# MLA head projections of a two-block model: rotations over both token tiles, a second query bank, the last heads' transposes moved behind the first scores

## The chip, the cores and the metric

One NeuronCore of one Trainium2 chip. The number reported is the device time of one execution in microseconds (us); several executions are summarised by their median. Lower is better.

## What is computed

The kernel computes two transformer blocks in a row on 256 tokens of width 1024, all in fp32. The second block has two layers: layer 0 with a sparse attention mixer (NSA), layer 1 with multi-head latent attention (MLA), and each layer ends in a mixture of 16 experts. The change is in layer 1's mixer:

```python
c_q = mix_cols[..., :MLA_Q_RANK]
c_kv = mix_cols[..., MLA_Q_RANK:MLA_Q_RANK + MLA_KV_RANK]
k_rope = mix_cols[..., MLA_Q_RANK + MLA_KV_RANK:]
q = (rms_norm_2(c_q, q_norm) @ w_uq).reshape(B, S, H, MLA_NOPE + MLA_ROPE)
q = jnp.concatenate([q[..., :MLA_NOPE], apply_rope(q[..., MLA_NOPE:], cos_m, sin_m)], -1)
kv = (rms_norm_2(c_kv, kv_norm) @ w_ukv).reshape(B, S, H, MLA_NOPE + MLA_V)
k_nope, v = kv[..., :MLA_NOPE], kv[..., MLA_NOPE:]
k_rope = apply_rope(k_rope[:, :, None, :], cos_m, sin_m)
k = jnp.concatenate([k_nope, jnp.broadcast_to(k_rope, (B, S, H, MLA_ROPE))], -1)
...
s = jnp.einsum('bqhd,bkhd->bhqk', qb, k) * scale
p = masked_softmax(s, mask)
```

The query rank is 256, the key/value rank 128, there are 12 heads, and of a head's 96 query and key columns the last 32 are rotated by position. After the mixer come an output projection with a residual and a layer norm, then the experts, whose weights (96 halves of 1 MB) are streamed from HBM.

## The kernel before

The program is written engine by engine: `tensor_program` (TensorE, PE in the profile), `vector_program` (VectorE, DVE), `scalar_program` (ScalarE, ACT), `pool_program` (GpSimd, POOL) and `sync_program` (the queue that issues the DMAs, SP). Each engine runs its list in order; semaphores tie the lists together. The 256 tokens are two tiles of 128 (t = 0, 1). PSUM has eight banks. `Banks.work` hands banks 0 to 3 out in turn to the named stages; `Banks.plan` names the banks. A stage's bank is claimed by TensorE (it waits until the last user's copy out of it is done), filled, and then emptied by DVE or ACT (`evac`).

The stretch around the change, in TensorE's order:

1. Stages `m` and `xq2` (L1674 to L1684): layer 1's input projection. `m` gives for each tile 416 columns (256 of c_q, 128 of c_kv, 32 of the key to be rotated), copied to the buffer `pm`; `xq2` is the query of the memory attention.
2. The root wait. ACT squares and sums both parts of both tiles of `pm` (L2972), DVE turns four sums into means (L2495), POOL takes the two inverse roots one after the other (L3029), and DVE multiplies the four parts by them (L2500). Only then does DVE rotate the key columns of tile 0 and of tile 1 (`rope`, L1849 to L1855, six instructions of 128x16 each).
3. Stages `cq` and `ck` (L1686 to L1694): six transposes, all four of `cq` into one bank; DVE copies both banks out with the gains (L2508, L1763).
4. `keep_on(psum[4], 7)` (L1726): seven matmuls of a constant on a constant, whose result nobody reads.
5. The head projections. Twelve heads are three parts of four. Step n (0 to 5) is part n // 2, the query for even n and key and value for odd n: `project(n)` fills banks `mp{n}`, one for each tile. For the query ACT copies tile 0 out and DVE tile 1, and DVE then rotates 4 heads x 16 column pairs of each tile (six instructions of 128x64 for each tile, L2525). For the key and value ACT does the copies (L2989, L2990), and POOL lays the rotated key beside every head (L3141). `turn_heads(n)` transposes the 96 columns of four heads back into banks `mt{n}`, two of them; ACT and DVE empty one each (`turned_heads`, 96x512). The transposes of step n - 2 come behind `project(n)`, those of steps 4 and 5 at the end. DVE and ACT also cut four pieces of the next weight matrix `ob0` into a high and a low half (`cast` on ACT L2597, then `cut` on DVE L1779), two before the loop and two at n == 1.
6. `attention(2)`: 8 turns of the loop over `c` for 12 MLA heads and 4 memory heads, and two turns to drain. In a turn TensorE makes four score tiles, transposes the probabilities of the turn before (`turn_probs`), and multiplies by the values. DVE adds the mask and takes the row minimum (`masks`), ACT takes the exponents, DVE the inverse sums, POOL scales the rows (L3039). Before the first score TensorE waits until banks 0 to 3 are empty. In the turn c == 1 it has another `keep_on(psum[7], 4)`.

The order on SP matters too. The first 23 expert halves of layer 1 are loaded ahead, each where its buffer comes free; of these the halves from n == 5 wait for s_pv 72, that is for the values of the last MLA heads (L903), and from n == 12 for the cut of `ob1` (L907). Once the experts run, a half is loaded whenever one has been used (L931).

## Time and profile before

| | us |
|---|---|
| median of 3 runs (lowest, highest) | 1025.46 (1024.38, 1026.41) |
| span of the profiled execution, first to last instruction | 1018.3 |
| median less that span | 7.2 |
| PE, DVE, ACT, POOL busy in the span | 977.9, 553.7, 410.1, 107.9 |
| HBM traffic over the span | 286 GB/s |

No time of the profiled execution is given beside its span. What lies around the span is taken as the 7.2 us by which the median is longer.

How to read it: a row of a timeline gives the start in us from the start of the span, the time in us until the group's last instruction ended, the engine, the source line, the operation, what is written and read with the shape, and how many instructions were merged (x4). In brackets stand the idle time just before it and who ended that. The table of windows gives for each stretch its length, then for PE, PEld (weight loads), DVE, ACT and POOL the busy time and the count of instructions, then TensorE's granted clock (1.00 is 2.4 GHz, 0.50 is 1.2 GHz), the share of the 16 DMA engines' time in which they were busy, and GB/s. Successive DVE instructions overlap, so their starts lie closer together than their durations say.

### The profile page before, as it was taken

The page shows a single profiled execution, that of the slowest core. Times are in us where ns is not written, and L with a number is a line of the kernel's source. Part 1 is how long each engine was busy: PE and PEld are TensorE (multiplying, and loading weights), DVE is VectorE, ACT ScalarE, POOL GpSimd, SP SyncE. Part 2 cuts the span into 40 slices and gives each one's busy share as a digit, 9 for nine tenths or more (in the row PEclk, how much of TensorE's full clock was granted, in tenths as well). Part 3 has the DMA queues.
Part 4 walks back from the last instruction along what each step waited for, and adds up shares of the span by engine and source line. Part 5 has one row for each costly group of instructions (what it writes and reads, how often), then busy time and mean ns, then how long its engine had stood idle before and what let it go on. Part 6 is the DMA issues. An engine that isn't in the chain of part 4 may idle for free.

```text
span 1018.3 us, 15420 instructions
## 1 busy us (share of the span) xinstructions
PE 977.9 (96%) x5850; PEld 666.7 (65%) x5850; DVE 553.7 (54%) x1201; ACT 410.1 (40%) x817; POOL 107.9 (11%) x143
## 2 busy tenths in 40 slices
PE   7999999999999999899999999989999999999995
PEld 7977899999886889777634334337777734343432
DVE  5766656676447744774523434366665613334374
ACT  5465456556436445683312122124474302221222
POOL 0721001111001100150001000000132001000000
PEclk9999999999999999999999999999999999999998
DMA  9882596556354543709999999997367999999994
GB/s 328 208 259 83 167 294 218 181 181 228 130 206 165 163 153 127 309 3 361 406 422 421 409 420 421 420 403 252 107 275 281 406 408 420 410 421 421 421 416 160
DMA packets 96686, 292.30 MB, mean 287 GB/s; under 512 B 11150, under 2 KB 48190, under 8 KB 73566
## 3 DMA queue, kind: packets, MB, share of 16 engines
q1 hardware_dynamic: 96606, 291.24, 75.2%
q8 instruction: 49, 0.80, 0.3%
q14 instruction: 31, 0.25, 0.1%
HBM read 289.98 MB, written 1.25 MB: 286 GB/s over the span
## 4 chain that ended last, share of the span: by engine, by line
PE 79%; DVE 8%; DMA 6%; ACT 3%; issue 2%; POOL 1%; SPq 0%; DVEq 0%; POOLq 0%; ACTq 0%
PE ps L1056 37%; PE ps L1517 16%; PE ps L1557 10%; DMA w<-in_moe_w_up 3%; DMA arena<-in_moe_w_up 3%; DVE yTr L2417 2%; PE ps L1165 2%; PE ps L1195 2%; PE ps L1176 2%; PE ps L1488 1%; PE ps L999 1%; DVE plo L1779 1%; PE ps L1567 1%; PE ps L1361 1%; PE ps L1605 1%
## 5 line engine op out<-in xcount | busy, mean ns | idle before, releaser
L1779 DVE TENSOR_TENSOR plo<-w,phi 128x1024 fp32r<-128x1024 f32 (+3 forms) x147 | 178.0, 1229 | 130.5 <-ACT phi L2597 130.2
L2597 ACT CAST phi<-w 128x1024 fp32r<-128x1024 f32 (+3 forms) x147 | 148.6, 1033 | 132.0 <-PE ps L1056 125.7
L2417 DVE SCALAR_TENSOR_TENSOR yTr<-ps,small,yTr 32x512 fp32r<-32x512 f32 x112 | 83.7, 748 | 179.6 <-ACT yTr L2896 177.9
L1517 PE MATMUL ps<-w,arena 128*64 128x512 f32 x464 | 135.6, 594 | 1.3 <-DMA w<-in_moe_w_up 1.3
L1056 PE MATMUL ps<-hTr,phi 128*128 128x256 f32 x472 | 131.5, 279 | 0.3 <-DVE yTr L1961 0.3
L1056 PE MATMUL ps<-hTr,plo 128*128 128x256 f32 x472 | 130.9, 277 | 0.0
L1056 PE MATMUL ps<-yTr,phi 128*128 128x256 f32 x472 | 130.9, 277 | 0.0
L1056 PE MATMUL ps<-phi,hTr 128*128 128x512 f32 (+2 forms) x240 | 93.8, 391 | 1.3 <-issue 0.7
L1056 PE MATMUL ps<-phi,yTr 128*128 128x512 f32 (+2 forms) x240 | 93.7, 390 | 0.7 <-DVE hTr L1771 0.7
L1056 PEld LDWEIGHTS ps<-hTr,phi 128*128 128x128 f32 x472 | 88.8, 188 | 0.6 <-issue 0.4
L1056 PEld LDWEIGHTS ps<-hTr,plo 128*128 128x128 f32 x472 | 88.9, 188 | 0.0
L1056 PEld LDWEIGHTS ps<-yTr,phi 128*128 128x128 f32 x472 | 88.7, 188 | 0.0
L1517 PE MATMUL ps<-arena 128*64 128x512 f32 x272 | 82.9, 595 | 1.5 <-DMA arena<-in_moe_w_up 1.5
L1517 PEld LDWEIGHTS ps<-w,arena 128*64 128x64 f32 x464 | 42.1, 137 | 62.8 <-issue 61.9
L1557 PE MATMUL ps<-w,ring 128*64 128x512 f32 (+1 forms) x296 | 78.6, 559 | 1.2 <-ACT ring L2920 0.7
L2896 ACT ACTIVATE yTr<-ps,small 128x512 fp32r<-128x512 f32 (+1 forms) x62 | 37.1, 674 | 98.6 <-PE ps L1557 90.5
L3029 POOL TENSOR_TENSOR small<-small 128x1 f32<-128x1 f32 (+1 forms) x18 | 11.5, 636 | 468.3 <-DVE small L1824 354.1
L1056 PE MATMUL ps<-plo,hTr 128*128 128x512 f32 (+2 forms) x144 | 55.4, 385 | 0.0
L1557 PEld LDWEIGHTS ps<-w,ring 128*64 128x64 f32 x296 | 26.9, 137 | 40.2 <-issue 37.3
L1056 PEld LDWEIGHTS ps<-phi,hTr 128*128 128x128 f32 x240 | 45.2, 188 | 11.8 <-issue 2.2
L1056 PEld LDWEIGHTS ps<-phi,yTr 128*128 128x128 f32 x240 | 45.2, 188 | 10.1 <-issue 1.4
L1517 PEld LDWEIGHTS ps<-arena 128*64 128x64 f32 x272 | 25.5, 137 | 39.9 <-issue 38.9
(372 smaller groups left out, 1729.8 us busy)
## 6 DMA issues: line engine op xcount, KB each, us to landing
w<-in_moe_w_up SPq DMA_DIRECT2D x31, 1024.0 KB, 18.0
w<-in_moe_w_down SPq DMA_DIRECT2D x30, 1024.0 KB, 17.4
w<-in_moe_w_gate SPq DMA_DIRECT2D x26, 1024.0 KB, 14.0
w<-in_w_up SPq DMA_DIRECT2D x22, 1024.0 KB, 7.8
arena<-in_moe_w_up SPq DMA_DIRECT2D x19, 1024.0 KB, 15.5
arena<-in_moe_w_gate SPq DMA_DIRECT2D x14, 1024.0 KB, 21.6
arena<-in_moe_w_down SPq DMA_DIRECT2D x13, 1024.0 KB, 18.7
w<-in_w_out SPq DMA_DIRECT2D x6, 2048.0 KB, 10.3
```

Of the source, the lines that this page charges most:

```text
L999: e.matmul(bank[:, 0:width], ident, mask if width == 256 else ident, start=True, stop=True)
L1056: ins_ = e.matmul(o, l[a], r[b], start=first and i == 0, stop=last and i == 2, skip_group_check=group)
L1165: ins_ = e.matmul(psum[2 * (u % 2) + j["half"]][:, q * 256:q * 256 + w], lq, kk, start=True, stop=True)
L1176: ins_ = e.transpose(bk[:, o * 128:o * 128 + 128], prob(j["J"])[:, c:c + 128], ident)
L1195: ins_ = e.matmul(ob[hp:hp + 64, t * 128:t * 128 + 128], *m[o], start=(o == 0), stop=(o == len(m) - 1))
L1517: ins_ = e.matmul(bank[64 * ee:64 * ee + 64, :], xg[:, k, o:o + 64], half_view(i, kind, p, ee, ab)[:, c, :], start=(k == 0), stop=(k == 7))
L1557: ins_ = e.matmul(bank[64 * ee:64 * ee + 64, :], turned[:, o:o + 64], down_view(i, p, ee, f, hf)[:, at], start=(f == 0), stop=(f == 3))
L1779: e.tensor_tensor(plo[:, 0:m], slots[u % 3][:, j * m:j * m + m], phi[:, 0:m].bitcast(F32), ALU.subtract).then_inc(s_cut)
L2417: ins_ = e.scalar_tensor_tensor(y_parts[t][other, part], psum[2 + hf][own_, :], slot_gate[own_, p:p + 1], y_parts[t][own_, part].bitcast(F ...
L2597: e.copy(pieces[p % 4][0][:, 0:m], slots[u % 3][:, j * m:j * m + m]).then_inc(s_cast)
L2896: ins_ = e.mul(y_parts[part][:, hf * 512 + at.start:hf * 512 + at.stop], bank[:, :], slot_gate[:, p:p + 1])
L3029: e.tensor_tensor(dst, dst, half_pow[:, 0:dst.shape[-1]], ALU.pow).then_inc(s_rstd)
```

## The change

- `cq` gets two banks, one for each half of the query rank. ACT empties the first, DVE the second; before, DVE emptied both halves. All later `work` stages move on by one bank.
- The key's rotation moves in front of the four multiplications by the inverse roots, and it is done over both tiles at once (`rope_tiles`, six instructions of 128x32). Tile 0's two multiplications stay on DVE, each waiting for its own root alone; tile 1's go to ACT. Before them ACT runs one Exp on a column, so that the Exp table is loaded there.
- Query rotations of a part go over both tiles at once (six instructions of 128x128 for twelve of 128x64), with scratch in `ring`.
- `keep_on(psum[4], 7)` becomes `keep_on(psum[4], 1)`, and the wait for `ck` moves to `project(1)`. `keep_on(psum[7], 4)` stays in layer 0's attention and is dropped from layer 1's.
- `turn_heads(4)` and `turn_heads(5)` move into the attention's turn c == 0, behind the first four score tiles, into banks 6, 7 and 4, 5; their copies on DVE stand behind `inverse_sums(0)`, on ACT behind the exponents of the second two tiles.
- The second pair of `ob0` pieces is cut at n == 0.

```diff
-        trq = [ar(64).rearrange("p (h d) -> p h d", h=4) for _ in range(4)]
+        trq = [ring[:, a:a + 128].rearrange("p (t h d) -> p t h d", t=2, h=4) for a in range(0, 512, 128)]
...
-        for stage, n in (("cq", 1), ("ck", 1)):
+        for stage, n in (("cq", 2), ("ck", 1)):
...
-        for n in (4, 5):
-            B.work(f"mt{n}", 2)
+        B.plan("mt4", 2, [6, 7])
+        B.plan("mt5", 2, [4, 5])
...
+                    if a == 2 and c == 0:
+                        turn_heads(4)
+                        turn_heads(5)
...
-                    if a and c == 1:
+                    if a == 1 and c == 1:
                         keep_on(psum[7], 4)
...
-            bk = claim("cq", 0)
             e.wait_ge(s_mnorm, 4)
-            for q in range(4):
-                ins_ = e.transpose(bk[:, q * 128:q * 128 + 128], pm[:, q % 2, (q // 2) * 128:(q // 2) * 128 + 128], ident)
-            ins_.then_inc(B.sem_full("cq", 0))
+            for c in range(2):
+                bk = claim("cq", c)
+                for t in range(2):
+                    ins_ = e.transpose(bk[:, t * 128:t * 128 + 128], pm[:, t, c * 128:c * 128 + 128], ident)
+                ins_.then_inc(B.sem_full("cq", c))
...
-            keep_on(psum[4], 7)
+            keep_on(psum[4], 1)
             e.wait_ge(*loaded("uq"))
             e.wait_ge(*loaded("ukv"))
-            await_empty("cq", "ck")
+            await_empty("cq")
             for n in range(6):
+                if n == 1:
+                    await_empty("ck")
                 project(n)
                 if n >= 2:
                     turn_heads(n - 2)
-            turn_heads(4)
-            turn_heads(5)
             attention(2)
...
+            def rope_tiles(x1, x2, lo, hi_, tmp, heads=0):
+
+                c, s = trig[:, 0, 0:2, lo:hi_], trig[:, 1, 0:2, lo:hi_]
+                if heads:
+                    c, s = (a.unsqueeze(2).broadcast_to([128, 2, heads, hi_ - lo]) for a in (c, s))
                 settle()
                 e.tensor_tensor(tmp[0], x1, c, ALU.mult)
                 e.tensor_tensor(tmp[1], x2, s, ALU.mult)
...
-            e.wait_ge(s_rstd, root.n)
             for t in range(2):
-                for n, (c0, w) in enumerate(((0, 256), (256, 128))):
-                    e.tensor_scalar(pm[:, t, c0:c0 + w], pm[:, t, c0:c0 + w], rsm[:, n, t:t + 1], None,
-                                    ALU.mult).then_inc(s_mnorm)
-            tr = [a[:, 0:16] for a in tmp4]
-            for t in range(2):
-                rope(pm[:, t, 384:400], pm[:, t, 400:416], t, 8, 24, [], tr).then_inc(s_mrope)
-                e.wait_ge(s_mrope, t + 1)
...
+                e.wait_ge(*B.empty("m", t))
+            tr = [a[:, 0:32].rearrange("p (t d) -> p t d", t=2) for a in tmp4]
+            rope_tiles(pm[:, :, 384:400], pm[:, :, 400:416], 8, 24, tr).then_inc(s_mrope)
+            for n, (c0, w) in enumerate(((0, 256), (256, 128))):
+                e.wait_ge(s_rstd, root.n - 1 + n)
+                e.tensor_scalar(pm[:, 0, c0:c0 + w], pm[:, 0, c0:c0 + w], rsm[:, n, 0:1], None,
+                                ALU.mult).then_inc(s_mnorm)
+            evac("cq", 1, cqT[:, 1, :], B.ap("cq", 1)[:, 0:256], colv[:, QN + 1:QN + 2])
             evac("ck", 0, ckT[:, 0, :], B.ap("ck", 0)[:, 0:256], colv[:, KN:KN + 1])
...
                 for t in range(2):
                     e.wait_ge(*B.empty(f"mp{n}", t))
-                    ins_ = rope(qk[:, t, :, 64:80], qk[:, t, :, 80:96], t, 8, 24, [4], trq)
-                    ins_.then_inc(s_qr)
-                    e.wait_ge(s_qr, 2 * part + t + 1)
+                rope_tiles(qk[:, :, :, 64:80], qk[:, :, :, 80:96], 8, 24, trq, 4).then_inc(s_qr)
...
+            e.wait_ge(s_msq, 4)
+            e.activation(table, ident[:, 0:1], ACT.Exp)
+            for n, (c0, w) in enumerate(((0, 256), (256, 128))):
+                e.wait_ge(s_rstd, 13 + n)
+                e.mul(pm[:, 1, c0:c0 + w], pm[:, 1, c0:c0 + w], rsm[:, n, 1:2]).then_inc(s_mnorm)
             evac("xq2", 0, xqT2, B.ap("xq2", 0)[:, :].rearrange("p (c t) -> p c t", c=2), -0.125,
                  used(first_piece("m1") + 3, 1))
+            evac("cq", 0, cqT[:, 0, :], B.ap("cq", 0)[:, 0:256], colv[:, QN:QN + 1])
...
-                if n == 1:
+                if n == 0:
                     cast(p0 + 2, p0 + 4)
```

## Rows read from the trace of the kernel before

**Rows 1.** Busy time, granted clock, DMA share and GB/s of three stretches to the end.

```profile
751.90:770.30 18.40, 17.36 (x156) 13.35 (x154) 14.10 (x69) 14.83 (x62) 9.57 (x11) 1.00 0.17 70
770.30:813.30 43.00, 41.65 (x244) 34.09 (x246) 22.95 (x64) 15.01 (x28) 3.96 (x5) 1.00 0.97 393
813.30:1002.00 188.70, 184.75 (x876) 71.05 (x872) 75.92 (x145) 35.31 (x60) 3.55 (x2) 1.00 1.01 412
```

**Rows 2.** Timeline of SP: the first DMA issue at the attention's end.

```profile
770.29 0.33 SPq L859 DMA_DIRECT2D arena<-in_moe_w_gate  x1
```

**Rows 3.** Timeline of the root wait, up to the first projection.

```profile
717.63 0.24 DVE L2495 TENSOR_SCALAR small<-small 128x2 f32<-128x2 f32 x2 [1.29 <-ACT ring L2972]
...
718.83 0.70 POOL L3029 TENSOR_TENSOR small<-small 128x2 f32<-128x2 f32 x1 [0.16 <-issue]
...
719.56 1.01 DVE L2500 TENSOR_SCALAR arena<-arena,small 128x256 f32<-128x256 f32 x4 [1.69 <-POOL small L3029]
...
720.14 0.28 PE L1056 MATMUL ps<-hTr,plo 128*128 128x256 f32 x1
...
720.72 0.63 PE L1689 MATMUL ps<-cst,arena 128*128 128x128 f32 x4 [0.29 <-DVE arena L2500]
...
720.95 1.98 ACT L2597 CAST phi<-w 128x1024 fp32r<-128x1024 f32 x2
...
721.40 3.19 PE L999 MATMUL ps<-cst 128*128 128x256 f32 x14
...
722.00 0.88 DVE L2508 TENSOR_SCALAR arena<-ps,colv 128x256 f32<-128x256 f32 x2
...
723.19 2.44 DVE L1779 TENSOR_TENSOR plo<-w,phi 128x1024 fp32r<-128x1024 f32 x2
```

**Rows 4.** The key/value weights: their issue on SP, and its time to landing.

```profile
716.37 0.34 SPq L777 DMA_DIRECT2D w<-in_mla_w_ukv  x1
...
w<-in_mla_w_ukv SPq DMA_DIRECT2D x1, 768.0 KB, 4.4
```

**Rows 5.** Timeline of TensorE in the projections and transposes.

```profile
724.42 2.75 PE L1704 MATMUL ps<-w,arena 128*128 128x384 f32 x8
...
736.21 0.64 PE L1723 MATMUL ps<-cst,arena 128*96 128x128 f32 x4 [1.15 <-DVE arena L1763]
...
742.87 0.64 PE L1723 MATMUL ps<-cst,hT 128*96 128x128 f32 x4 [0.41 <-DVE arena L1763]
743.35 1.91 PE L1723 MATMUL ps<-cst,arena 128*96 128x128 f32 x16
```

**Rows 6.** Timeline of DVE: evacuation, rotation, evacuation.

```profile
732.89 0.55 DVE L1761 COPY hT<-ps 128x384 f32<-128x384 f32 x1
...
733.36 0.21 DVE L1849 TENSOR_TENSOR arena<-hT,small 128x64 f32<-128x64 f32 x1
...
735.47 0.69 DVE L1763 TENSOR_SCALAR arena<-ps 96x512 f32<-96x512 f32 x1
```

**Rows 7.** Timeline of DVE in layer 0's rotation, instructions of 128x96.

```profile
385.75 0.25 DVE L1849 TENSOR_TENSOR small<-arena,small 128x96 f32<-128x96 f32 x1
```

**Rows 8.** Timeline of the attention's first two turns, TensorE and POOL.

```profile
746.08 2.00 PE L1165 MATMUL ps<-arena 96*128 96x128 f32 x12 [0.83 <-DVE arena L1761]
...
749.59 1.04 POOL L3039 TENSOR_TENSOR ring<-ring,small 128x512 f32<-128x512 f32 x1 [0.28 <-DVE small L1893]
...
751.48 0.60 PE L1176 MATMUL ps<-cst,ring 128*128 128x128 f32 x4
```

**Rows 9.** Timeline of ACT where the Exp table was loaded early on.

```profile
56.21 1.28 ACT L2720 ACT_TABLE_LOAD   x1
57.51 0.20 ACT L2720 ACTIVATE small<-cst 128x1 f32<-128x1 f32 x1
```

**Rows 10.** Busy time and granted clock of two stretches at the end.

```profile
1008.00:1012.00 4.00, 0.00 (x0) 0.00 (x0) 3.84 (x7) 2.84 (x10) 1.22 (x3) 1.00 0.02 6
1012.00:1018.30 6.30, 0.00 (x0) 0.00 (x0) 2.36 (x4) 0.00 (x0) 0.40 (x1) 0.59 0.48 177
```

29 lines of the change are left out of this document (17 added, 12 removed).

## The prediction

> **What bounds the kernel now.** I read the table of windows first, to find what sets the end. From 813.3 to 1002 us the DMA engines are busy for the whole stretch (share 1.01, 412 GB/s), and from 770.3 to 813.3 nearly so (0.97), while from 751.9 to 770.3 they are almost idle (0.17) [rows 1]. So the end is a stream of expert weights that starts at one instant and runs at the rate of the DMA engines. The timeline of SP gives that instant: the first issue after the idle stretch is at 770.29, and in the code it waits for the values of the last MLA heads (s_pv 72, L903) [rows 2]. All later issues of the stream wait for work behind that attention, so an attention that ends x us earlier should move the whole tail by x. In the stretch before it there is DMA idle time on one side and a chain over three engines on the other: whatever shortens the chain is worth its full length.
>
> The chain is read from the timeline, in three pieces: the root wait up to the first projection at 724.42 [rows 3, 5], the projections, in which TensorE twice waits for a DVE evacuation (1.15 us before 736.21, 0.41 before 742.87) [rows 5], and the attention from 746.08, whose second turn puts its last transposes at 751.48 [rows 8].
>
> **The change, part by part.** Times are those of the profiled execution; I compute new instants on the same axis.
>
> *Root wait.* Now DVE multiplies from 719.56, when the second root is there (718.83 + 0.70), to 720.57, and the transposes start at 720.72 although TensorE had issued its last product at 720.14 [rows 3]. The rotation stands behind the multiplications and holds the first evacuation of `cq` until 722.00. In the new order DVE rotates both tiles between 717.87 and about 718.7, under POOL's roots, and multiplies tile 0's two parts at about 718.7 and 719.6. ACT multiplies tile 1's. The Exp table load begins behind the squares at 717.63; the earlier load took 1.28 us and its Exp 0.20 [rows 3, 9], so ACT is free at 719.1 and its second product, which waits for the root at 719.53, ends at about 719.9. That is before TensorE is free, at about 720.3: these additions cost nothing, cover 0.4 us. With some 0.2 us for the waits TensorE starts transposing at 720.5 (0.2 gained). The second `cq` bank is full at 721.15, DVE empties it by 721.6 (0.44 for each, rows of 722.00 [rows 3]) and `ck` by 722.1. ACT empties the first after `xq2`, by 721.4, and then casts two pieces (0.99 each, now from 720.95, then from 721.4) until 723.4 [rows 3]. One dummy matmul instead of seven takes 0.46 us in place of 3.19 [rows 3]. The first projection starts at 721.8 in place of 724.42: 2.6 earlier, all of it time that TensorE spent in dummies or waiting.
>
> The Trainium skill, "ScalarE: Activation LUTs", section "What ACT_TABLE_LOAD costs", speaks against the placing: it puts a drain of about 1380 ns on top of the load. With that, tile 1 would be multiplied at 721.1, after TensorE is free, and the start of the transposes would be 0.6 us later. In this trace the Exp behind the load begins at 57.51, 1.30 us after the load did at 56.21, with no drain to be seen between them [rows 9]. I take the trace's value.
>
> *Do the weights arrive?* The last load needed is issued at 716.37 and lands 4.4 us later, at 720.8 [rows 4]. That issue does not move. It leaves 1.0 us before 721.8, where the dummies used to cover 3.6.
>
> *Projections up to the second key transposes.* Here DVE is the longest list. It cuts two pieces (1.22 each [rows 3]) from 722.45, as ACT's casts end, to 724.9; the second query tile's evacuation costs 0.47 until the next instruction can start (732.89 to 733.36 [rows 6]); then the rotation. Now two rotations take 2.11 us (733.36 to 735.47 [rows 6]), that is 1.05 for six instructions. The new one has six of 128x128. No row shows that width in a rotation. Six instructions of 128x64 last 0.21 each and one of 128x96 0.25 [rows 6, 7]: 0.035 for 32 columns more, so about 0.07 more each at 128, and 1.05 + 6 x 0.07 = 1.47. Bounds: 1.05, if width costs nothing, and 2.11, if the tile dimension makes it cost as much as two. I take 1.47, the nearest rows being the ones extrapolated; each rotation gains 0.64. The list then runs: evacuation and rotation to 726.9, two cuts to 729.35, evacuation and rotation to 731.35, first transposed evacuation (0.69 [rows 6]) to 732.05. TensorE's second key transposes, which wait for exactly that, start at 732.15 in place of 736.21: 4.05 gained. TensorE's own list would be there at about 732.0: of the 11.8 us from 724.42 to 736.21 it waited 1.15 [rows 5] and some 0.45 for the evacuation of 732.89 [rows 6], and 10.2 of work from 721.8 remain. So both lists arrive together, and a gain on one alone would be lost.
>
> The second pair of casts on ACT (2.0 us) moves in front of the first key evacuations; these are needed only at 731.9 and end at 727.0. Cost nothing. If that cover is gone it is 1 us.
>
> *Second round.* From 736.21 to 742.87 is 6.66 us [rows 5]; projection, evacuation, rotation and transposed evacuation follow each other in it, and one rotation gains 0.64: 6.0 us, so the last key transposes of part 1 start at 738.15, 4.7 gained. POOL's key copies now start at about 720.5, and part 2's wait for the second key transposes; none is late.
>
> *The attention's start.* Now sixteen transposes follow (1.91 us from 743.35) with their evacuations, and the first score is at 746.08 [rows 5, 8]. Now it will need only the evacuation of the transposes at 738.15: 0.68 to its start, 0.69, 0.1, thus 739.65. That is 6.4 earlier.
>
> *The first two turns.* The sixteen transposes (1.7 us of issue) now stand between the first and second pairs of scores, and four `keep_on` matmuls (1.7 us) are gone. TensorE's sum does not change; the wait does. Relative to the first score, the transposes of the second tile pair start at 5.4 (751.48) [rows 8]. New: behind scores and transposes TensorE has the last scores done at 4.3. Its wait for POOL's second scaling runs through DVE's list: DVE empties the two moved banks at 2.45 to 3.05 and 3.25 to 3.95, takes the minima of the third tile pair until 4.35, then the inverse sums until 4.5; POOL scales for 1.04 [rows 8] from 4.75 to 5.8. So the transposes start at 5.85: 0.45 lost. ACT's two extra copies (1.0 us) delay its third exponents to 4.2; not on that path. Bounds of this loss: 0, if DVE's copies fall in its idle time, and 1.4, if both 0.69 copies [rows 6] come in full on POOL's path. From the third turn on TensorE's own work fills the turns as before.
>
> **The sum.** 2.6 (start) + 1.45 (DVE list with one rotation shorter and less idle) + 0.65 (second rotation) + 1.7 (the last transposes and evacuations out of the way: 6.4 - 4.7) - 0.45 = 5.95 us. Against the span: 1018.3 - 5.95 = 1012.3; the median lies 7.2 above the span, so 1019.5 from 1025.46.
>
> **The rivals.**
>
> *B, the moved heads hurt the first turns.* The evacuations sit in three in-order lists ahead of the first softmax. If the loss is at its bound of 1.4 and the rotation at its bound of 2.11 (0.64 x 2 lost), the gain is 5.95 - 0.95 - 1.3 = 3.7: 1021.8. For it: DVE and TensorE are both tight there. Against: TensorE waited 0.83 before the scores, and its issue count doesn't grow [rows 8].
>
> *C, the tail does not follow.* If the stream were set by something outside this chain, the 6 us would reappear as DMA wait: 1025. Against: the DMA engines stand idle for 83% of the 18.4 us before 770.3 [rows 1]. Little is left for it.
>
> *D, slower: TensorE's clock falls.* Ten dummy matmuls go, 4.4 us of TensorE's activity. If the granted clock drops to its lower level over the first turns, the matmul time there doubles. The place is 739.7 to 749.7, with about 9.4 us busy, so 9.4 lost against 5.95 gained: 1029. It decides from 6 us of matmuls at 1.2 GHz on. For it: at the very end the clock is 0.59 with no matmul [rows 10]. Against: the 4.0 us without any matmul just before still show 1.00, and the longest wait left in the new chain is well under 1 us. The Trainium skill, "TensorE: Matmul & The Clock Gate", section "Part 1: The HAM clock gate", says that the low clock is the default and only activity releases it. By this rule, the trace agrees only at the end.
>
> *E, the weights hold the projection.* If the load lands 1.5 us later than in this execution, the first projection starts at 722.3, and about 0.5 us of the gain goes: 1020.0. It lies inside the range.
>
> **How the numbers follow.** Forecast with E 0.78, B 0.12, C 0.05, D 0.05. Predicted 1019.5. The range goes from 1017.5 (the rotation at its lower bound, 0.8, no loss in the first turns, 0.45, and 0.75 for the spread of the runs) to 1022.8 (B, plus 1.0 for that spread). About 0.2% (2 us) is what a measurement can tell from no change; the forecast and B are both beyond it: faster 0.90. C is the same, 0.05; D is slower, 0.05.
>
> **What would show it.** Right: the first projection at about 721.8, the first score at about 739.7, rotations of six 128x128 instructions near 0.29 us, `s_pv` issue near 764.3 with DMA shares after it unchanged, the clock at 1.00 throughout. Wrong: a gap between the last input product and the transposes (table load), TensorE waiting on DVE in the attention's second turn by more than 0.5 us, DMA share under 0.95 in the tail, or a first DMA issue that is 6 us earlier and an end that is not.

## The result and the profile after

The changed kernel takes 1016.13 us (median of six executions, 1013.12 to 1018.1) against 1024.78 us for the kernel before, timed beside it on the same chip (six executions, 1020.13 to 1026.41). The ratio is 0.9924, with an interval of 0.9904 to 0.9945. The forecast was 1019.5 with a range from 1017.5 to 1022.8: direction right, time missed, on the low side. Most executions of either kernel fall into two groups some 4 to 5 us apart, so a median of a few depends on how many of each it holds.

The profiled execution took 1014.59 us, with a span of 1012.7 us. The span forecast was 1012.3. The timeline of TensorE from the last input product to the first turns of the attention, with SP's first issue behind them, answers to [rows 3, 5, 8, 2]. Its columns are start, us, engine, line, operation, tiles, form, count, and the idle time before with its releaser.

```profile
720.33 0.28 PE L1056 MATMUL ps<-hTr,plo 128*128 128x256 f32 x1
720.57 0.63 PE L1693 MATMUL ps<-cst,arena 128*128 128x128 f32 x4
...
721.25 0.60 PE L999 MATMUL ps<-cst 128*128 128x256 f32 x2
721.97 2.82 PE L1708 MATMUL ps<-w,arena 128*128 128x384 f32 x8
...
731.51 1.04 PE L1727 MATMUL ps<-cst,arena 128*96 128x128 f32 x8
...
737.56 1.05 PE L1727 MATMUL ps<-cst,hT 128*96 128x128 f32 x8
739.58 1.55 PE L1165 MATMUL ps<-arena 96*128 96x128 f32 x8 [0.98 <-DVE arena L1765]
740.97 1.91 PE L1727 MATMUL ps<-cst,arena 128*96 128x128 f32 x16
...
745.45 0.63 PE L1176 MATMUL ps<-cst,ring 128*128 128x128 f32 x4 [1.03 <-POOL ring L3058]
...
764.36 0.33 SPq L859 DMA_DIRECT2D arena<-in_moe_w_gate  x1
```

Two waits are missing and two remain. Both sets of key transposes now run as unbroken groups of eight. In the kernel before, the second four of each set waited, 1.15 and 0.41 us [rows 5]. What is left is 0.98 us in front of the first score and 1.03 us in the attention's second turn, for POOL's scaling (L3058).

The gain by stages, each difference between two instants of one kernel, then compared. The second four of a group of eight are taken to start four times 0.11 us (731.62 less 731.51, the first two starts) behind the first.

| Stage | before, us | after, us | gain | forecast |
|---|---|---|---|---|
| last input product to first projection | 4.28 | 1.64 | 2.64 | 2.6 |
| to second key transposes | 11.79 | 9.98 | 1.81 | 1.45 |
| to last key transposes of part 1 | 6.66 | 6.05 | 0.61 | 0.65 |
| to first score | 3.21 | 1.58 | 1.63 | 1.7 |
| to last transposes of second turn | 5.40 | 5.87 | -0.47 | -0.45 |
| to first issue of the stream | 18.81 | 18.91 | -0.10 | 0 |
| sum | 50.15 | 44.03 | 6.12 | 5.95 |

The whole length from the last input product to the end of the span went from 298.16 us (1018.3 less 720.14) to 292.37 (1012.7 less 720.33): 5.79 of the 6.12 us reach the end. The table of windows shows why, and answers to [rows 1, 10]. Its columns are the stretch, its length, busy time and instructions of TensorE, its weight loads, DVE, ACT and POOL, the granted clock as a share of full speed, the DMA share and GB/s.

```profile
745.90:764.40 18.50, 17.42 (x156) 13.35 (x154) 14.05 (x69) 14.87 (x62) 9.80 (x12) 1.00 0.29 121
764.40:807.40 43.00, 41.66 (x244) 34.04 (x246) 22.92 (x62) 14.99 (x28) 3.93 (x5) 1.00 0.96 393
807.40:996.30 188.90, 184.66 (x875) 70.95 (x872) 75.90 (x145) 35.30 (x60) 3.55 (x2) 1.00 1.01 411
1002.30:1006.30 4.00, 0.05 (x1) 0.00 (x0) 3.84 (x7) 2.84 (x10) 1.16 (x3) 0.90 0.02 6
1006.30:1012.70 6.40, 0.00 (x0) 0.00 (x0) 2.44 (x4) 0.00 (x0) 0.47 (x1) 0.50 0.47 173
```

The tail is the same stream at the same rate (0.96, then 1.01), only earlier. TensorE is nearly as busy in it as the DMA engines, 184.66 of 188.9 us; which of the two sets the pace is taken up with the held stream below. The DMA engines' idle stretch before it is busy for 0.29 where it was 0.17, probably because it now lies 6 us nearer to the transfers that were issued ahead of the attention.

### The profile page after: what moved, and what is told of

The parts are those of the page before. It is cut to its first block, busy times and chain, and to the rows that moved or that the text cites. A ratio compares the mean times of both kernels' runs of the same rounds, so it can differ in the third digit from the quotient of the medians.

```text
span 1012.7 us, 15351 instructions
## 1 busy us (share of the span) xinstructions
PE 973.5 (96%) x5830; PEld 663.4 (66%) x5830; DVE 550.6 (54%) x1174; ACT 412.0 (41%) x821; POOL 107.4 (11%) x143
## 4 chain that ended last, share of the span: by engine, by line
PE 81%; DVE 7%; DMA 6%; ACT 3%; issue 2%; POOL 1%; SPq 0%; DVEq 0%; POOLq 0%; ACTq 0%
PE ps L1056 37%; PE ps L1520 16%; PE ps L1560 10%; DMA w<-in_moe_w_up 3%; DMA arena<-in_moe_w_up 3%; DVE yTr L2438 2%; PE ps L1195 2%; PE ps L1165 2%; PE ps L1176 2%; PE ps L1491 1%; PE ps L999 1%; PE ps L1570 1%; PE ps L1364 1%; PE ps L1708 1%; PE ps L1608 1%
## 5 line engine op out<-in xcount | busy, mean ns | idle before, releaser
L1056 PE MATMUL ps<-hTr,phi 128*128 128x256 f32 x472 | 131.2, 278 | 0.0
L1056 PE MATMUL ps<-hTr,plo 128*128 128x256 f32 x472 | 130.7, 277 | 0.0
L1056 PE MATMUL ps<-yTr,phi 128*128 128x256 f32 x472 | 130.7, 277 | 0.0
L1056 PE MATMUL ps<-phi,hTr 128*128 128x512 f32 (+2 forms) x240 | 93.6, 390 | 1.3 <-issue 0.7
L1056 PE MATMUL ps<-phi,yTr 128*128 128x512 f32 (+2 forms) x240 | 93.4, 389 | 0.5 <-DVE hTr L1775 0.5
L1056 PEld LDWEIGHTS ps<-yTr,phi 128*128 128x128 f32 x472 | 88.8, 188 | 0.0
L1056 PEld LDWEIGHTS ps<-hTr,plo 128*128 128x128 f32 x472 | 88.7, 188 | 0.0
L1056 PEld LDWEIGHTS ps<-hTr,phi 128*128 128x128 f32 x472 | 88.6, 188 | 0.1
L1056 PE MATMUL ps<-plo,hTr 128*128 128x512 f32 (+2 forms) x144 | 55.1, 383 | 0.0
L1056 PEld LDWEIGHTS ps<-phi,hTr 128*128 128x128 f32 x240 | 45.1, 188 | 11.6 <-issue 2.2
L1056 PEld LDWEIGHTS ps<-phi,yTr 128*128 128x128 f32 x240 | 45.1, 188 | 9.8 <-issue 1.2
```

Of the source, the lines that this page charges most:

```text
L1056: ins_ = e.matmul(o, l[a], r[b], start=first and i == 0, stop=last and i == 2, skip_group_check=group)
```

## The experiments

Executions are compared by distances inside one trace, counted from the first query transposes (T0). Up to the last input product just before T0 TensorE's work is the same in every kernel, yet T0 lies between 720.1 and 725.9 us. T0 itself moves with the root wait: it comes 0.58 us behind that product before the change and 0.24 after it, so distances from T0 leave out 0.34 us of the gain. For the changed kernel T0 is 720.57, the first score follows 19.01 us later, the second turn's last transposes 24.88, the stream's first issue 43.79, the `out` issue (L951, 1006.03) 285.46 and the end of the span 292.13. For the kernel before, with T0 at 720.72 [rows 3], the first score comes at 25.36, those transposes at 30.76, the first issue at 49.57 and the end at 297.58.

### The changed kernel again

No edit: it gives the spread, and a second and a third comparison.

> The changed kernel once more, against the kernel before in five rounds on one chip. In the two profiled executions the chain gained 5.9 us at the attention's end (770.29 to 764.36) and the span 5.6. Theory 1 (the chain gives 5.6 to 6 us, and what the medians show beyond it, 8.65 us, is the mixture of executions some 4 us apart that both kernels have): the medians on one chip lie 5 to 7 us apart, the fastest executions too, and time less span is 1.9 us in each. Theory 2 (the change also shortens something that these two profiles don't show, or makes the longer executions rarer): medians 8 to 10 us apart.

> The changed kernel a third time, as the yardstick for the next kernel on the same chip. If the longer executions differ from the shorter ones by a slower pitch of the first block's up projection alone, which both kernels share, then the executions of this kernel and of the kernel before each fall into two groups 4 to 5 us apart, and the groups of the one lie 5 to 7 us below those of the other.

The first gave 1015.42 us against 1024.38, a ratio of 0.9932 (0.9908 to 0.9956); its trace has T0 at 720.66, and behind it 19.02, 24.88, 43.75 and 292.54 us (score, transposes, issue, end). The second, on a different chip, gave 1018.45 against 1024.48, 0.9949 (0.9932 to 0.9966), with 19.02, 24.88, 43.73 and 291.86 us. The distances agree within 0.1 us up to the issue, and the end within 0.7 us (291.86 to 292.54), while the medians of three measurements of one kernel lie 3 us apart. So the distances up to the issue can tell steps of some tenths apart, the end of the span only steps of about 1 us, and a median of a few executions not even that.

The first expectation came in only in part. The medians lie 8.96 us apart, where theory 1 had 5 to 7 and theory 2 had 8 to 10; in the other comparison they lie 6.03 apart. The fastest executions are 5.43 us apart and time less span is 1.9 us, as theory 1 had it. Four of six executions of the changed kernel and six of fifteen of the kernel before were of the shorter group (two of the six, 1021.72 and 1022.45, lie between the groups); in the other comparison it was two of eight and one of eleven. Taken group by group, the means differ by 5.8 us in both groups, in the other comparison by 6.1 in the shorter and 5.6 in the longer. So the 8.96 holds the mixture, and nothing shows that the change makes either group rarer.

### Seven dummy matmuls back

```diff
-            keep_on(psum[4], 1)
+            keep_on(psum[4], 7)
```

> The changed kernel with seven dummy matmuls in front of the projections again. Theory 1: TensorE's projections start at 724.6 instead of 721.97, DVE's first evacuation moves from 724.85 to 727.4, and as both lists have no room after that, the first score comes 2.5 us later (742.1) and the span is 2.5 us longer (1015.2). Rival (DVE's list alone sets the projections, and TensorE's start has room): first score under 0.5 us later.

Timeline of TensorE, then of DVE and SP:

```profile
720.88 0.63 PE L1693 MATMUL ps<-cst,arena 128*128 128x128 f32 x4
...
724.58 2.74 PE L1708 MATMUL ps<-w,arena 128*128 128x384 f32 x8
...
727.36 0.56 DVE L1765 COPY arena<-ps 128x384 f32<-128x384 f32 x1 [2.12 <-PE ps L1708]
...
766.84 0.34 SPq L859 DMA_DIRECT2D arena<-in_moe_w_gate  x1
```

The first projection comes 3.70 us behind T0 in place of 1.40, and 2.23 of these 2.30 us are still there at the first score (21.24), 2.17 at the first issue (45.96) and 2.5 at the end. DVE, which has no such wait in the changed kernel, stands idle for 2.12 us before its first evacuation. Timed, it is 1017.17 against 1024.38: 0.9948 (0.9927 to 0.9969). So the dummies lay on the path in their full length, and the end follows within its spread of 0.7. They are the largest single part of the gain.

### The last heads' transposes back in front

```diff
-        B.plan("mt4", 2, [6, 7])
-        B.plan("mt5", 2, [4, 5])
+        for n in (4, 5):
+            B.work(f"mt{n}", 2)
...
-                    if a == 2 and c == 0:
-                        turn_heads(4)
-                        turn_heads(5)
...
+            turn_heads(4)
+            turn_heads(5)
             attention(2)
```

and the same for the evacuations on DVE and ACT.

> The changed kernel with the last heads' sixteen transposes and their evacuations in front of the attention again; the dummies of its second turn stay out. Theory 1: the first score 1.75 us later (741.3), but in the second turn TensorE's last transposes start 4.65 us behind the first score instead of 5.87, as POOL's scaling is ready that early: net 0.5 us later. So nearly all that the move gained is that it could replace dummies. Rival (the move itself is worth the 1.75 us): net 1.2 us later or more.

Timeline of TensorE (T0 is 724.49), then SP's first issue:

```profile
745.25 2.00 PE L1165 MATMUL ps<-arena 96*128 96x128 f32 x12 [0.98 <-DVE arena L1764]
...
749.95 0.63 PE L1176 MATMUL ps<-cst,ring 128*128 128x128 f32 x4 [0.88 <-POOL ring L3055]
...
768.80 0.34 SPq L859 DMA_DIRECT2D arena<-in_moe_w_gate  x1
```

The first score comes 20.76 us behind T0, 1.75 later than with the move; but the second turn's transposes follow 4.70 us behind it in place of 5.87, and the first issue comes at 44.31, only 0.52 later. The end of this one trace lies 1.18 us later (293.31), 0.8 to 1.5 against the three traces of the changed kernel, so at the end the 0.5 us expected and the rival's 1.2 can't be told apart. Up to the issue, the move buys 1.75 us and the second turn gives 1.17 of them back. The forecast had 1.7 for the first. Its 0.45 of loss was counted against the kernel before, in whose second turn four dummies stood as well; against the same turn without them the moved heads cost 1.17.

### Without the second turn's dummies alone

The kernel before, with one line of the change:

```diff
-                    if a and c == 1:
+                    if a == 1 and c == 1:
                         keep_on(psum[7], 4)
```

> The kernel before with one line of the change alone: no dummy matmuls in the second turn of layer 1's attention. Theory 1: TensorE then waits for POOL's second scaling, which ends 4.55 us behind the first score; the last transposes of that turn start 4.65 us behind it instead of 5.40, so everything behind comes 0.75 us earlier (first issue behind the attention 48.8 us after the query transposes instead of 49.6). Rival (the granted clock falls without them): a clock below 1.00 in the attention and a later end.

The first score stands at 25.38 us behind T0 (before: 25.36), the second turn's last transposes at 30.07 (30.76) and the first issue at 48.92 (49.57). So these four dummies cost 0.69 us at the transposes and 0.65 at the issue (at the end 0.35, less than its spread), and the transposes then wait for POOL (T0 is 725.87):

```profile
755.94 0.63 PE L1176 MATMUL ps<-cst,ring 128*128 128x128 f32 x4 [0.87 <-POOL ring L3039]
```

The granted clock is 1.00 from 750.0 to 758.0 us, around the first two turns, and its mean over the execution stays at 0.997. The two experiments close the account of the second turn: 0.69 gained, 1.17 lost, -0.48 together, where the table has -0.47.

### A rotation for each tile

```diff
-                rope_tiles(qk[:, :, :, 64:80], qk[:, :, :, 80:96], 8, 24, trq, 4).then_inc(s_qr)
+                for t in range(2):
+                    ins_ = rope(qk[:, t, :, 64:80], qk[:, t, :, 80:96], t, 8, 24, [4], [a[:, t, :, :] for a in trq])
+                    if t == 0:
+                        own.step(ins_)
+                    else:
+                        ins_.then_inc(s_qr)
```

> The changed kernel with each part's query rotation done for tile 0 and then for tile 1 (twelve instructions of 128x64, scratch as in the change). Theory 1: each rotation 0.65 us longer, two of them on the path: first score 1.2 to 1.3 us later (740.8), of the second TensorE waits in the key transposes as before the change. Rival (TensorE's own list sets the pace and DVE has room): under 0.4 us later.

Timeline of DVE in the changed kernel, one rotation and the next item of its list:

```profile
724.85 0.55 DVE L1765 COPY arena<-ps 128x384 f32<-128x384 f32 x1
725.49 0.29 DVE L1867 TENSOR_TENSOR ring<-arena,small 128x128 f32<-128x128 f32 x1
...
726.64 0.28 DVE L1873 TENSOR_TENSOR arena<-ring 128x128 f32<-128x128 f32 x1
726.84 2.35 DVE L1783 TENSOR_TENSOR plo<-w,phi 128x1024 fp32r<-128x1024 f32 x2
```

The same with a rotation for each tile, and what it does to TensorE:

```profile
730.45 0.23 DVE L1853 TENSOR_TENSOR ring<-arena,small 128x64 f32<-128x64 f32 x1
...
732.32 0.22 DVE L1859 TENSOR_TENSOR arena<-ring 128x64 f32<-128x64 f32 x1
732.45 2.35 DVE L1783 TENSOR_TENSOR plo<-w,phi 128x1024 fp32r<-128x1024 f32 x2
...
736.47 0.60 PE L1727 MATMUL ps<-cst,arena 128*96 128x128 f32 x4
738.10 0.64 PE L1727 MATMUL ps<-cst,arena 128*96 128x128 f32 x4 [1.03 <-DVE arena L1767]
```

A rotation of both tiles takes 1.35 us (725.49 to 726.84), two of one tile take 2.00 (730.45 to 732.45): 0.65 each, and 0.29 for an instruction of 128x128, the value extrapolated in the forecast. But the first score comes 1.91 us later (746.44 less T0 at 725.52, 20.92 in place of 19.01) and the first issue 1.85 later. That is three rotations, not the two (1.2 to 1.3 us) that I expected. DVE's list up to the second key transposes holds the rotations of n = 0 and n = 2 and both count; the third is in the round behind. The rows bear this out: the second key transposes come 1.20 us later than in the changed kernel (12.58 behind T0 in place of 11.38), and the round behind them is 0.67 longer. The end is 1.45 us later. In the changed kernel TensorE waits for none of them; here the wait of 1.03 us before 738.10 is back.

### The root wait as before

All four multiplications on DVE behind the second root, the rotation behind them:

```diff
+            e.wait_ge(s_rstd, root.n)
+            for t in range(2):
+                for n, (c0, w) in enumerate(((0, 256), (256, 128))):
+                    e.tensor_scalar(pm[:, t, c0:c0 + w], pm[:, t, c0:c0 + w], rsm[:, n, t:t + 1], None,
+                                    ALU.mult).then_inc(s_mnorm)
             rope_tiles(pm[:, :, 384:400], pm[:, :, 400:416], 8, 24, tr).then_inc(s_mrope)
...
-            for n, (c0, w) in enumerate(((0, 256), (256, 128))):
-                e.wait_ge(s_rstd, 13 + n)
-                e.mul(pm[:, 1, c0:c0 + w], pm[:, 1, c0:c0 + w], rsm[:, n, 1:2]).then_inc(s_mnorm)
```

> The changed kernel with the root wait in its old order: DVE makes all four multiplications when both roots are there, and rotates the key behind them (both tiles at once); ACT makes none. Theory 1: the transposes start 0.15 us later, DVE's copy of the second query bank about 0.2 us later, while DVE's next work (the cuts) waits for ACT's casts in either order: the first score comes 0.1 to 0.3 us later. Rival (the key's rotation in the root wait carries the gain in front of the projections): first score 0.9 us later or more. As the start of the transposes itself moves, it is counted from the end of the input projection's last product.

Timeline of TensorE, ACT and DVE, merged by start:

```profile
725.35 0.63 PE L1693 MATMUL ps<-cst,arena 128*128 128x128 f32 x4 [0.51 <-DVE arena L2524]
...
725.80 0.47 ACT L2586 ACTIVATE arena<-ps,colv 128x256 f32<-128x256 f32 x1 [0.33 <-PE ps L1693]
...
726.17 1.98 ACT L2610 CAST phi<-w 128x1024 fp32r<-128x1024 f32 x2
...
727.24 2.45 DVE L1783 TENSOR_TENSOR plo<-w,phi 128x1024 fp32r<-128x1024 f32 x2 [0.34 <-ACT phi L2610]
```

Here T0 itself moves, so I count from the last input product (724.56). The transposes come 0.79 us behind it in place of 0.24, and the first score 19.81 in place of 19.25: 0.56 us. I expected 0.1 to 0.3, with the rotation covered. The rotation is covered, but the late transposes are not: ACT's evacuation waits for them, the casts stand behind it in ACT's order, and DVE's cuts wait for the first cast (0.34 us). DVE's list starts 2.68 us behind the last product in place of 2.24 (722.57 less 720.33). At the first issue 0.63 us of it is left (44.66 in place of 44.03).

### The query rows in one bank

The four query transposes go to one bank, which DVE empties with both halves, as before the change:

```diff
-            for c in range(2):
-                bk = claim("cq", c)
-                for t in range(2):
-                    ins_ = e.transpose(bk[:, t * 128:t * 128 + 128], pm[:, t, c * 128:c * 128 + 128], ident)
-                ins_.then_inc(B.sem_full("cq", c))
+            bk = claim("cq", 0)
+            for q in range(4):
+                ins_ = e.transpose(bk[:, q * 128:q * 128 + 128], pm[:, q % 2, (q // 2) * 128:(q // 2) * 128 + 128], ident)
+            ins_.then_inc(B.sem_full("cq", 0))
```

> The changed kernel with the four query transposes in one bank, both halves emptied by DVE. Theory 1: DVE's three copies end 0.45 us later and the first projection starts 0.2 to 0.45 us later; ACT's casts come 0.35 us earlier, so DVE's list behind it does not start later; TensorE's list and DVE's tie, so the first score comes 0.2 to 0.4 us later. Rival (DVE's list alone sets the pace): first score unchanged or 0.1 us earlier.

```profile
725.09 0.63 PE L1692 MATMUL ps<-cst,arena 128*128 128x128 f32 x4
...
726.89 0.88 PE L1707 MATMUL ps<-w,arena 128*128 128x384 f32 x2 [0.52 <-DVE arena L2527]
```

In this timeline the first projection waits 0.52 us for DVE's second half (L2527) and starts 1.80 us behind T0 in place of 1.40. At the first score 0.26 us of the 0.40 are left (19.27), at the first issue 0.37 (44.16), as expected; at the end (292.41) it is lost in the spread. The second bank is worth its 0.3 to 0.4 us probably because only one dummy is left to cover an evacuation: in the kernel before, DVE's last of the three copies ended at 723.28 while the dummies ran until 724.59. No run had both seven dummies and one bank.

### The stream held back

```diff
-                        e.wait_ge(s_pv, (40, 72)[i])
+                        e.wait_ge(s_pv, (40, 80)[i])
```

> The changed kernel with the issue of the weight half n == 5 held until s_pv 80 (the last values of all heads) in place of 72. Nothing on the compute engines is touched. Counted from the first query transposes, the first issue behind the attention moves from 43.8 to about 52.6 us. Theory (the tail is a stream that runs at the rate of the DMA engines from that issue on): the end moves by 7 to 9 us, the DMA engines' share staying near 1.0 behind it. Rival (TensorE's chain sets the end, and the stream only keeps up with it): the end moves by less than 1 us.

Timeline of SP:

```profile
772.79 0.34 SPq L859 DMA_DIRECT2D arena<-in_moe_w_gate  x1
...
1012.46 0.36 SPq L951 DMA_DIRECT2D out<-x  x1
```

Nothing of the computation in front of the stream moves: the first score stays at 19.02 us behind T0 (721.12). The first issue comes at 51.67, 7.9 us later, the `out` issue at 291.34, 5.9 later, and the end at 298.38, 6.2 later. So the end does depend on the instant of that issue, and the rival by which it moves under 1 us falls. But it is not one to one: I expected 7 to 9 us at the end, and 1.6 of the 7.9 us were absorbed (2.0 at the `out` issue).

The rows show where. First an issue far down the stream in the changed kernel, then the same and the next ones with the stream held:

```profile
879.42 0.33 SPq L859 DMA_DIRECT2D arena<-in_moe_w_gate  x1
```

```profile
879.93 0.45 SPq L859 DMA_DIRECT2D arena<-in_moe_w_gate  x1
880.42 7.25 SPq L859 DMA_DIRECT2D w<-in_moe_w_gate  x3
```

Behind T0 that issue stands at 158.85 us and, held, at 158.81. So from about 62 us behind T0 up to here, 115 us behind the first issue of the changed kernel, the issues are where they were: each waits for TensorE to use a half. Only from here on do the held issues take longer (7.25 us for the three that take 3.86 in the changed kernel) and TensorE wait for weights. Its waits for a DMA from 764 us to the end, the longest group of either trace (total, times, longest in us), first the changed kernel and then held:

```profile
PE ps L1520 <- DMA w<-in_moe_w_up: 1.3, 1, 1.3
```

```profile
PE ps L1520 <- DMA w<-in_moe_w_up: 3.3, 3, 1.3
```

All such waits together are 2.3 us in the changed kernel and 7.7 held, and none of them lies before 879 us in either. So in the changed kernel the tail is not the stream alone: for much of it TensorE's own work sets when halves are issued, and as far as this one run shows, the stream is late enough to hold the end only when its start is moved by more than about 2 us. An earlier attention moves both. No run moved TensorE's work without the stream.

### The inverse sums between the moved evacuations

The 1.03 us wait in the second turn goes back to DVE: it makes POOL's inverse sums only behind both moved evacuations and the minima of the third tile pair. Here they stand between the two evacuations:

```diff
-                    if 1 <= c <= n:
+                    if 1 <= c <= n and not (a == 2 and c == 1):
                         inverse_sums(2 * c - 1)
...
                         turned_heads(4)
+                        inverse_sums(1)
                         turned_heads(5)
```

> The changed kernel with DVE's inverse sums of the second pair of score tiles put between the two moved evacuations of the first turn (they stood behind the second one and behind the third pair's minima). Theory 1: POOL's second scaling is what TensorE waits 1.03 us for in the second turn; the sums can start at 3.2 us behind the first score instead of 4.36, the scaling ends at 4.6, and the last transposes start at about 4.75 instead of 5.87: everything behind 1.0 to 1.1 us earlier, span about 1 us shorter in executions with the same start. Rival (TensorE or ACT are as late anyway): under 0.3 us earlier.

Timeline of POOL, ACT and TensorE in the second turn (T0 is 720.12):

```profile
742.65 1.04 POOL L3059 TENSOR_TENSOR ring<-ring,small 128x512 f32<-128x512 f32 x1 [0.28 <-DVE small L1911]
...
744.19 0.24 ACT L2648 COPY ring<-ps 128x128 f32<-128x128 f32 x1
...
744.49 0.77 PE L1176 MATMUL ps<-cst,ring 128*128 128x128 f32 x4 [0.52 <-ACT ring L2648]
```

POOL is done at 743.69, 22.53 + 1.04 us behind T0, and no longer the last. Yet the transposes come only 0.51 us earlier (24.37), where I expected 1.1. They now wait for ACT's copy of the first turned tile, which stands behind the exponents of the third tile pair and both moved evacuations in ACT's order. The wait changed its owner: DVE's list and ACT's list had both grown by the two evacuations, and only one had been unburdened. The first issue is 0.42 us earlier, and the end (292.08) no earlier than in the changed kernel, where I expected 1 us. Timed, 1015.88 against 1020.87: 0.9942 (0.9921 to 0.9962), which tells nothing against the changed kernel's 0.9932 and 0.9949.

### Only one of the two heads behind the score

The transposes of step 4 go back in front of the attention, where TensorE waits 0.98 us for an evacuation anyway; the inverse sums come directly behind step 5's evacuation.

```diff
                     if a == 2 and c == 0:
-                        turn_heads(4)
                         turn_heads(5)
...
                     turn_heads(n - 2)
+            turn_heads(4)
             attention(2)
...
                     if a == 2 and c == 0:
-                        turned_heads(4)
                         turned_heads(5)
+                        inverse_sums(1)
```

ACT's list changes in the same way, and `inverse_sums(1)` is left out at its old place, as in the experiment above.

> The changed kernel with step 4's transposes back in front of the attention, where TensorE waits 0.98 us anyway, and with DVE's inverse sums of the second pair of score tiles directly behind its one moved evacuation. Theory 1: first score unchanged (19.0 us behind the query transposes), POOL's second scaling done at 4.55 us behind it, ACT's copy of the first turned tile at about 4.5, so the last transposes of the second turn start at about 4.65 instead of 5.87, and all behind comes 1.2 us earlier: first issue behind the attention at 42.6 us, span 1.2 us shorter for the same start. Rival (the first score moves back by TensorE's 0.86 us of transposes or by the additional copies): gain under 0.4 us.

Timeline of TensorE (T0 is 723.81), then SP's first issue:

```profile
742.82 1.55 PE L1165 MATMUL ps<-arena 96*128 96x128 f32 x8
744.21 1.04 PE L1726 MATMUL ps<-cst,arena 128*96 128x128 f32 x8
...
747.51 0.63 PE L1176 MATMUL ps<-cst,ring 128*128 128x128 f32 x4 [0.58 <-ACT ring L2648]
...
766.36 0.34 SPq L859 DMA_DIRECT2D arena<-in_moe_w_gate  x1
```

The first score stays at 19.01 us behind T0 and has no wait in front of it: eight transposes fill the 0.98 us. The second turn's transposes follow it by 4.69 us in place of 5.87, the first issue comes at 42.55 in place of 43.79, and the end at 291.29 in place of 292.13. Timed, it is 1016.84 against 1024.48, a ratio of 0.9916 (0.9893 to 0.9938), beside 0.9949 (0.9932 to 0.9966) for the changed kernel in the same comparison. The intervals overlap, but taken group by group the executions don't, two against two and four against six: 1012.92 and 1013.02 against 1013.97 and 1014.25, and 1016.78 to 1017.55 against 1018.24 to 1019.89. So this version is faster than both kernels, over the changed one by 1.24 us at the first issue and by 0.6 to 1.2 at the end of the span, against its three traces.

## Why the prediction was right, and where it was wrong

**The step that failed** is the last of the sum: "the median lies 7.2 above the span, so 1019.5 from 1025.46". It sets a span of one execution against a median of others. The time of an execution lies 1.8 to 2.0 us above its own span in every one of which both are known (1014.59 and 1012.7, 1021.02 and 1019.1, 1024.97 and 1023.1). The profiled execution of before, whose time wasn't shown, had a span of 1018.3 and so took about 1020.2 us, not 1025.46; the three executions whose times were shown (1024.38 to 1026.41) were all of the other kind. The difference of 5.3 us was not an overhead to be added, but the distance between two groups of executions. Of the 17 executions of before timed beside the inverse sums nine took 1019.55 to 1020.87 us and eight 1024.36 to 1025.89. The twelve of the two medians shown at the result hold both kinds as well: before 1020.13 and 1020.64 beside 1024.38 to 1026.41, after 1013.12 to 1014.59 beside 1017.68 to 1018.1.

So 1019.5 was in effect a forecast for the longer group alone, and the 0.75 us that the range allowed for the spread of the runs knew of one group, while the six executions of the changed kernel spread over 5 us. The measured median, 1016.13, is the middle between the slowest of the shorter group and the fastest of the longer. Of the 3.4 us by which it lies below the forecast, 1.7 are this mixture; the longer group's own median, 1017.84, is 1.7 below the forecast and would have been in the range. Whether the time fell in the range was thus also a matter of how many executions of each group were drawn.

In which stretch the two groups part can be read from the thirteen traces. The same line of the first block's up projection (L1056), in code that no kernel here changes, has matmuls of two durations. Columns: operation, tiles, count, minimum, median and maximum in ns, first and last start. First the kernel before, whose profile is of the short kind; then the experiment with a rotation for each tile, of the long kind.

```profile
L1056 PE MATMUL ps<-hTr,plo x295: 275/277/277, 134.8 to 234.8; 128*128 128x256 f32 x148
```

```profile
L1056 PE MATMUL ps<-hTr,plo x284: 281/281/281, 134.8 to 234.8; 128*128 128x256 f32 x142
```

In the same 100 us the one kind issues 295 matmuls with these operands and the other 284, 3.7% fewer, at a granted clock of 1.00 in both. Seven traces show 276 or 277 ns and have T0 between 720.1 and 721.1; six show 281 and have T0 between 723.8 and 725.9. From its first to its last such matmul the up projection takes 119.3 to 119.4 us in the seven and 124.0 to 124.1 in the six, while from there to the last input product it is 473.8 to 475.0 us in all thirteen. So 4.6 to 4.8 us between the two kinds arise in this one stretch. The code of the line is the same in every program, and both kernels have times in both groups; but no single program was traced in both kinds. Forecast and result should have been held against each other in one group: 1014.2 (a span of 1012.3 and 1.9) against 1014.59 for the profiled execution, 0.4 us apart. In the long group the forecast would have been 1025.2 - 5.95 = 1019.3 against 1017.7 to 1018.1 here and 1018.2 to 1019.9 in the repeats. The 7.5 us between the long groups' means in this comparison did not come again: the repeats have 5.8 and 5.6, and the short groups 6.4, 5.8 and 6.1. The step was open to doubt beforehand: an excess of 7.2 us over the span was taken without asking what it was made of.

**The steps of the sum** stand, with a measured size for each.

- *Start, 2.6*: 2.64 measured. Singly: 2.30 for the dummies, 0.55 for the multiplications and rotation taken apart, 0.40 at the first projection for the second bank. They add to more than 2.64, probably since they cover one another: behind seven dummies the second bank would have had nothing to save.
- *The weights*: the load still takes 4.3 us and is there in time (rival E falls): TensorE waits for nothing before 721.97.
- *DVE's list, 1.45*: 1.81 measured. The sum calls this term "DVE list with one rotation shorter", but its working counts both of the list's rotations, at 1.47 us each, and ends the list at 732.05. It ended at 731.79, although the last input product came 0.19 later than in the kernel before. The rotation took 1.35, two cuts 2.28 from start to start in place of 2.44, the evacuation in front of a rotation 0.64 in place of 0.47. TensorE has no wait left in this stretch, so it is now its own work that sets the 9.98 us, for which the forecast had 10.2 (it took the wait for the evacuation of 732.89 as 0.45; the trace has 0.30). The separate rotations account for 1.20 of the 1.81 us. Part of the rest may be the earlier cutting of the second pair of `ob0` pieces, which no run tested alone: in the kernel before, DVE stood idle for 0.85 us for ACT's casts, and in the changed one it does not.

```profile
730.61 2.36 DVE L1779 TENSOR_TENSOR plo<-w,phi 128x1024 fp32r<-128x1024 f32 x2 [0.85 <-ACT phi L2597]
```

- *Second round, 0.65*: 0.61, and 0.67 with a rotation for each tile.
- *Last transposes out of the way, 1.7*: 1.63, and 1.75 taken singly.
- *First two turns, -0.45*: -0.47, made of 0.69 gained and 1.17 lost. Rival B had the mechanism with a loss of 1.4; the moved heads did cost 1.17, but the removed dummies paid for more than half of it. TensorE's wait in the second turn, 1.03 us, is above the 0.5 us that the prediction named as a sign of being wrong. The wait is for POOL, held up by DVE's list, and the sum had it.
- *The tail follows one to one*: 5.79 of 6.12 us, and 5.4 and 6.1 against the two repeats. Rival C falls by this. But the reason given, a stream that runs at the rate of the DMA engines from its first issue, is half of it: the held stream shows TensorE's own work setting the issues up to 115 us behind the first one, and 1.6 us of a late start absorbed.

**The clock** (rival D). In the chain it is 1.00 everywhere, with waits up to 1.03 us and ten dummies fewer. At the very end the clock does fall, where it costs nothing: in the 4 us before 1006.3, with one matmul of 0.05 us, the granted clock is 0.90, and behind them 0.50, the lower level (1.2 GHz) throughout; before, the like stretches had 1.00 and 0.59 [rows 10]. So the 4 us of idle time that I had named as safe are not always so. The Trainium skill, "TensorE: Matmul & The Clock Gate", section "Part 1: The HAM clock gate", makes the low clock the default that only activity lifts; by this rule, the trace agrees at the end, and nowhere in the chain does it bite.

**The table load.** The timeline of ACT in the changed kernel:

```profile
717.82 1.28 ACT L2989 ACT_TABLE_LOAD   x1
719.11 0.20 ACT L2989 ACTIVATE small<-cst 128x1 f32<-128x1 f32 x1
719.22 0.49 ACT L2992 ACTIVATE arena<-arena,small 128x256 f32<-128x256 f32 x1
719.91 0.40 ACT L2992 ACTIVATE arena<-arena,small 128x128 f32<-128x128 f32 x1 [0.19 <-POOL small L3048]
```

The next instruction starts 1.29 us behind the start of the load, the multiplication 0.11 behind that, and tile 1 is done at 720.31, before TensorE is free. The drain of about 1380 ns that the Trainium skill, "ScalarE: Activation LUTs", section "What ACT_TABLE_LOAD costs", puts on top of the load is not in this trace. By that figure, as an estimate, tile 1 would have been done at about 721.4 and the transposes some 0.8 us later than they were. The row's value was the right one.

## What to carry to other kernels

Set a sum against the time of the execution it was read from: here span and time differ by 1.8 to 2.0 us in every execution, and the larger excess of the median meant that the trace and the median belonged to different kinds of executions. Then look at single times and not at the median alone. Dummy matmuls put in to keep the clock up are free only as long as something else holds the engine; once the wait they filled gets shorter, they are the wait, and the first thing to measure. Work moved out of a serial stretch into a pipelined one is entered in every in-order list that serves it: move as much as fills the wait it leaves behind (here one of two heads), and let the item that the farthest engine waits for go first in each list, not in one alone.

## What the runs showed of the hardware

- Matmuls of one form, 128x256 in the first block's up projection, last 276 ns in seven of the thirteen traces and 281 in six, over the whole 100 us read, at a granted clock of 1.00 both times. In the six, one of the three weight loads in turn also lasts 192 ns in place of 187. The stretch takes 4.6 to 4.8 us longer with it. What picks the kind was not found; the line's code is the same in all of them.
- A DVE instruction's time against its width, in this kernel: 0.21 to 0.23 us at 128x64 and 0.28 to 0.29 at 128x128. Twice the width costs about a third more, and a rotation of both tiles takes 1.35 us where two of one tile take 2.00.
